# Dropping 16 learned rows behind the token mixers, folding the last token tile, and one ring of 16 slots for all expert weights

## The chip, the cores and the metric

One core of a Trainium2 chip runs the whole program; nothing is computed on the host. The metric is the device time of one execution in microseconds (us). Engines are named as in the profile: PE (TensorE, matmuls), PEld (its weight loads), DVE (VectorE), ACT (ScalarE), POOL (GpSimd), SP (SyncE, which here only issues DMAs, in the order in which they are written).

## What is computed

One layer of a hybrid decoder step, in float32, for one prompt of 256 tokens with 16 learned tokens ahead of it (272 rows), and 8 sample sequences of 8 tokens (64 rows): 336 rows of width 1024.

```
hp = concatenate([meta, x_prompt]);  hs = x_sample
h += W_out( sigmoid(g_A) * P_A(RWKV7(xn)) + sigmoid(g_B) * P_B(FoX(xn)) ),   xn = RMSNorm(h)
hp = hp[:, 16:]                                # the learned rows are dropped here
h += HierMoE(RMSNorm(h))                       # top 1 of 4 groups, then top 2 of its 8 experts
y = RMSNorm(h)
```

Each of the 32 experts is `silu(x @ w1) * (x @ w3) @ w2` with an inner width of 256; its weights are 3 MB (w1 and w3 side by side in two parts, w2 as a third). The learned rows are needed in the mixers (the prompt attends to them, and their keys and states are returned), but nothing behind the mixers returns them.

## The kernel before

The 336 rows are tokens in three tiles, `ROWS = [128, 128, 80]`: tile 0 begins with the 16 learned rows, tile 2 holds the last 16 prompt rows and the 64 sample rows. The program is a row of blocks with a barrier between them: *proj* (projections), *rwkv_pre*, *rwkv* (levels, samples, pairs, chunks), *rwkv_post*, *cache* (attention of the samples over 16 pages each, with 64 MB of page loads), *merge* (from 619 us) and *moe* (from 724 us).

The gates g_A and g_B are 16 blocks of 128 x 336, one for each `gate_mm` (8 float32 matmuls, each two instructions, L222). They are spread over *rwkv_pre* (6), the levels (4), the samples (2), the pairs (2) and *rwkv_post* (2), where they fill gaps on PE; ACT copies each to a stage and SP writes it to `gates_dram`. *cache* reads them back.

*merge*, in PE's order: the merged rows mT (L1910, 8 blocks, `gate` and `obT` against the two projections; DVE multiplies by the sigmoids, POOL adds), then `out_proj(0)`, `out_proj(1)`, `turn_x2(0)`, the first half of `out_proj(2)`, `logits(0)`, `turn_x2(1)`, its second half, `logits(1)`, `turn_x2(2)`, `logits(2)` (L1923, L1939, L1950). On DVE `residual(i)` adds the input (L2042), `norm(i)` makes x2 (L2048 clears the unused rows of tile 2, L2055 multiplies), with the sum of squares and the root on ACT (L1986, L1989). Behind `logits(2)` a chain of some 40 small DVE operations picks the experts, with a mask `tokmask` for the learned rows and the empty ones, and PE counts the tokens of each expert (L1969, L1972).

*moe* takes the experts in 8 quads of 4 (`NQD`, `QE`), with room for 32 tokens each (`CAP`). In PE's order for quad q: `hidden(q, 0)` (L2222, w1 and w3's first half of rows, 4 experts on 32 columns of the array each), `scatter(q-1)` (L2237, the tokens' results into two banks, which DVE adds to h2, L2415), `hidden(q, 1)`, `gather_quad(q+1)` (L2202, x2 by a 0/1 matrix), `outputs(q)` (L2245, L2256, w2). Tokens beyond an expert's 32 are done in passes of one expert each: after `hidden(3, 1)` (`OVQ = 3`) PE, ACT and DVE run `overflow(p)` n_pass times (L2273 to L2299, L2463). n_pass is read from a table that DVE makes at the stage's start (`ovt_ready`).

Loads of the weights. `expert_load(q, part, j)` brings 1 MB into a slot. There are 16 slots; the order is (q, part, j), 12 loads a quad. The first 16 go to slots 0 to 15, 12 of them and (1, 0, j) in *merge*, as its own weights are used up. From the 17th on the slot is `(n - 16) % 12`. Before each load SP waits until the slot's last user is done (`freed`): `w13a_used` or `w13b_used` for parts 0 and 1, the second `y_ps` of the quad for part 2. The pass's loads go to slots 12 to 14 (`ow`), behind (3, 2, 3) in SP's order (L2180).

The end: after the last `outputs` and `scatter(7)` DVE adds, ACT squares, DVE scales (L2503), and SP writes y_p and y_s.

Of the kernel before, what the change touches and what calls it, by code (L numbers as in the profile page):

```python
# [21 lines left out]
NE = NG * EPG  # L22
# [7 lines left out]
ATILES = AP_ // P  # L30
ZC = 1 + LP + DB * (1 + DS)
# [10 lines left out]
MAXOV = 2 * (T - NMETA) // (CAP + 1)  # L42

# [48 lines left out]
def build(nc, A, O):  # L92
# [17 lines left out]
    with ctx:  # L110
# [95 lines left out]
        gates_dram = nc.dram_tensor("gates_dram", (2 * (DM // P), P, T), f32, kind="Internal").ap()  # L206
# [535 lines left out]
        with nc.Block("rwkv_pre") as block:  # L742
# [81 lines left out]
            def _(act):  # L824
                def gate_out(j):
# [3 lines left out]
                    nc.scalar.activation(stage[j % 2], bank[6 + j % 2][:, 0:T], ACT.Copy).then_inc(S("gt_sb"), 1)  # L829
# [158 lines left out]
        with nc.Block("rwkv_pairs") as block:  # L988
# [272 lines left out]
            def _(act):  # L1261
# [19 lines left out]
                def gate_out(j, b):  # L1281
# [4 lines left out]
                    cp(stage[j % 2], bank[b][:, 0:T]).then_inc(S("w_gt_sb"), 1)  # L1286
# [164 lines left out]
        with nc.Block("rwkv_post") as block:  # L1451
# [90 lines left out]
            def _(act):  # L1542
                def gate_out(j):
# [4 lines left out]
                    nc.scalar.activation(stage[j % 2], bank[6 + j % 2][:, 0:T], ACT.Copy).then_inc(S("p_gt_sb"), 1)  # L1548
# [69 lines left out]
        gsb = Space(arena, free_k, mark_k1)(NGT, T)  # L1618
# [213 lines left out]
        mT = sp6(KT, T)  # L1832
        sp6 = Space(arena, free_k, tail - SLOT)
        h2 = sp6(NT, DM)
        mark6 = sp6.at
        sp6.at += NGT * T - NT * DM
        tga, tgb = (sp6(2, T) for _ in range(2))
        mark_t = sp6.at
        xt6 = sp6(NT, DM)
        lnb2 = sp6(DM)  # L1840
        mfills = [f + 16 for f in cache_fills]
# [3 lines left out]
        x2 = sp7(NT, DM)  # L1845
        x2T = xnT
# [5 lines left out]
        tokmask = sp7(NT)  # L1852
# [19 lines left out]
        with nc.Block("merge") as block:  # L1872
            @block.sync
            def _(sp):
                sp.dma_start(xt6[0:NMETA, 0, :], A["meta"]).then_inc(S("xr_in"), 16)
                sp.dma_start(xt6[NMETA:P, 0, :], A["xp"][0:P - NMETA, :]).then_inc(S("xr_in"), 16)
                sp.dma_start(xt6[:, 1, :], A["xp"][P - NMETA:2 * P - NMETA, :]).then_inc(S("xr_in"), 16)
                sp.dma_start(xt6[0:NMETA, 2, :], A["xp"][2 * P - NMETA:SEQ, :]).then_inc(S("xr_in"), 16)
                sp.dma_start(xt6[NMETA:ROWS[2], 2, :], A["xs"]).then_inc(S("xr_in"), 16)
# [11 lines left out]
                for j in range(QE):  # L1891
                    if j < QE - 1:
                        sp.wait_ge(S("out_k"), 2 * j + 2)
                    else:
                        sp.wait_ge(S("ho_ps"), 2 * NT)
# [3 lines left out]
            def _(pe):  # L1899
                for d in range(ND):  # L1900
# [7 lines left out]
                    for a, src in enumerate((gate, obT)):  # L1908
                        for k in range(4):
                            mm = nc.tensor.matmul(bank[b0 + a][:, 0:T], w[:, d % 2, a, k, :], src[:, k, :],  # L1910
                                                  start=(k == 0), stop=(k == 3))
                        mm.then_inc(S("mg_ps"), 1)
                def out_proj(i, ks):
                    r = ROWS[i]
                    for k in ks:
# [6 lines left out]
                        for half in range(2):  # L1922
                            mm = nc.tensor.matmul(bank[2 * i + half][0:r, :], mT[:, k, i * P:i * P + r],  # L1923
                                                  w[:, k % 2, half * 512:(half + 1) * 512],
                                                  start=(k == 0), stop=(k == KT - 1))
                            if k == KT - 1:
                                mm.then_inc(S("ho_ps"), 1)
# [5 lines left out]
                def turn_x2(i):  # L1933
                    n = ROWS[i]
                    pe.wait_ge(S("x2_ready"), i + 1)
                    for half in range(2):
                        for k in range(4):
                            kk = 4 * half + k
                            mm = nc.tensor.transpose(bank[tbank[i] + half][:, k * P:k * P + n],  # L1939
                                                     x2[0:n, i, kk * P:(kk + 1) * P], ident[0:n, 0:n])  # L1940
                        mm.then_inc(S("x2T_ps"), 1)

                def logits(i):
                    n = ROWS[i]
# [15 lines left out]
                out_proj(2, range(KT // 2, KT))  # L1960
                logits(1)
                turn_x2(2)
# [4 lines left out]
                for i in range(NT):  # L1967
                    for k in range(i + 1):
                        nc.tensor.matmul(bank[7][:, i * NE:(i + 1) * NE], tri_tok if k == i else ones, fe(k),  # L1969
                                         start=(k == 0), stop=(k == i))  # L1970
                for k in range(NT):
                    mm = nc.tensor.matmul(bank[7][:, NT * NE:(NT + 1) * NE], ones, fe(k),  # L1972
# [4 lines left out]
            def _(act):  # L1977
# [6 lines left out]
                for i, n in enumerate(ROWS):  # L1984
                    act.wait_ge(S("h2_sb"), 2 * i + 2)
                    nc.scalar.activation(jk[0:n, i, :], h2[0:n, i, :], ACT.Square,  # L1986
                                         accum_out=ss[0:n, i:i + 1]).then_inc(S("ss2"), 1)
# [3 lines left out]
                    nc.scalar.activation(x2T[:, 4:8, i * P:i * P + n],  # L1991
                                         bank[(6, 0, 2)[i] + 1][:, :].rearrange("p (k t) -> p k t", k=4)[:, :, 0:n],
                                         ACT.Copy).then_inc(S("x2T_b"), 1)
# [6 lines left out]
            def _(pool):  # L2000
# [11 lines left out]
                ch(nc.gpsimd.memset(tokmask, 1.0))  # L2012
# [566 lines left out]
```

## Time and profile before

| | |
|---|---|
| three runs | 989.3 us median, 983.65 to 995.3 |
| profiled execution | 986.92 us, of it the span 985.3 |
| PE | busy 819.0 us, 83% of the span |
| DVE, ACT, POOL | 361.7, 188.9, 153.4 us |
| granted PE clock | 0.899 of full |
| DMA | 219.01 MB, mean 222 GB/s |
| expert weights | 99 loads of 1 MB |
| *merge* and *moe* | from 619 us to the end |

Busy shares are means over stages with different limits, so they don't say what bounds the kernel. Readings below are by stretches. A float32 matmul is two instructions in the profile, so a count of x32 is 16 matmuls. Times are from the span's start.

### The profile page before, as it was taken

Reading aid. Unit: us, or ns where it says so; the run is one execution under the profiler, and the core shown is the slowest. Engines: PE = TensorE matmul, PEld = TensorE weight load, DVE = VectorE, ACT = ScalarE, POOL = GpSimd, SP = SyncE. Lnnn points to the kernel's source line nnn. Section 1 sums busy time; section 2 is a strip of 40 time slices with the busy share of each in tenths; the row PEclk is TensorE's granted clock in tenths of the full one; section 3 lists DMA queues with packets and bytes.
Section 4 is the critical chain, followed back from the end, with each engine's and each line's share of the span. In section 5 each row is a group of like instructions: output and inputs, shape, how many; then the busy total and the mean of one; then the engine's idle time right before and its main releaser. Section 6 shows DMA issues by size and latency. Waiting matters only on the chain. (4 is left out here: it accounts for less than half of the span.)

```text
span 985.3 us, 20675 instructions
## 1 busy us (share of the span) xinstructions
PE 819.0 (83%) x8683; PEld 489.6 (50%) x8683; DVE 361.7 (37%) x666; ACT 188.9 (19%) x430; POOL 153.4 (16%) x299
## 2 busy tenths in 40 slices
PE   4999899989689898666586886899769997899885
PEld 2445566655566577433364554564454444444321
DVE  2002433379422443548675640112352221422223
ACT  3003121143312110221131121301111110111012
POOL 8200110060400200500344443120000000000000
PEclk9999899979789699787878897899869998999998
DMA  8422232213203032166999999962409999399993
GB/s 332 180 85 89 86 102 80 86 39 114 78 21 103 10 92 69 60 197 210 376 415 413 396 380 388 365 252 89 171 1 407 421 422 424 160 391 420 422 422 124
DMA packets 48694, 219.01 MB, mean 222 GB/s; under 512 B 17567, under 2 KB 21962, under 8 KB 24026
## 3 DMA queue, kind: packets, MB, share of 16 engines
q1 hardware_dynamic: 41440, 186.03, 49.0%
q0 software_dynamic: 6512, 31.48, 8.2%
q8 instruction: 68, 1.11, 0.4%
q10 hardware_dynamic: 650, 0.18, 0.1%
q14 instruction: 24, 0.20, 0.1%
HBM read 210.96 MB, written 6.70 MB: 221 GB/s over the span
## 5 line engine op out<-in xcount | busy, mean ns | idle before, releaser
L222 PE MATMUL bank<-arena 128*128 128x336 f32 x256 | 85.7, 477 | 4.0 <-PEq L108 4.0
L2415 DVE TENSOR_TENSOR arena<-arena,bank 128x512 f32<-128x512 f32 (+1 forms) x48 | 32.9, 686 | 122.4 <-PE bank L2237 121.7
L1448 DVE STREAM_TRANSPOSE arena<-arena 128x2048 f32<-128x2048 f32 x32 | 72.3, 2289 | 10.0 <-DMA arena<-in_ck 8.9
L197 POOL DMA_DIRECT2D arena<-in_cv x112 | 58.0, 518 | 105.1 <-PE bank L1711 76.4
L495 PE MATMUL bank<-arena 128*128 128x336 f32 x224 | 70.4, 470 | 4.4 <-DVE arena L641 4.4
L2222 PE MATMUL bank<-arena 128*32 128x512 f32 x512 | 66.7, 608 | 7.2 <-DMA arena<-in_w_exp 6.5
L1711 PE MATMUL bank<-arena 128*16 128x128 f32 x1024 | 41.4, 329 | 33.9 <-issue 16.5
L2202 PE MATMUL bank<-arena 128*128 128x128 f32 x432 | 56.1, 294 | 9.7 <-DVEq L2452 5.6
L2202 PEld LDWEIGHTS bank<-arena 128*128 128x128 f32 x432 | 54.4, 209 | 16.6 <-issue 7.2
L222 PEld LDWEIGHTS bank<-arena 128*128 128x128 f32 x256 | 48.3, 199 | 27.7 <-issue 8.9
L474 PE MATMUL bank<-arena 128*128 128x512 f32 (+1 forms) x144 | 62.1, 593 | 0.0
L1670 PE MATMUL bank<-arena 32*32 32x512 f32 x1024 | 46.8, 737 | 17.0 <-DVE arena L1448 8.6
L495 PEld LDWEIGHTS bank<-arena 128*128 128x128 f32 x224 | 43.6, 199 | 27.2 <-issue 9.5
L1711 PEld LDWEIGHTS bank<-arena 128*16 128x16 f32 x1024 | 33.9, 115 | 39.9 <-DMA arena<-in_cv 18.3
L1262 ACT ACTIVATE arena<-bank 128x384 f32<-128x384 f32 (+6 forms) x63 | 26.1, 445 | 126.7 <-PE bank L222 47.4
L2237 PE MATMUL bank<-arena 128*128 128x512 f32 x96 | 46.9, 618 | 0.6 <-ACT arena L2375 0.6
L1910 PE MATMUL bank<-arena 128*128 128x336 f32 x128 | 39.5, 473 | 4.7 <-PEq L108 4.7
L474 PEld LDWEIGHTS bank<-arena 128*128 128x128 f32 (+1 forms) x144 | 25.4, 177 | 35.9 <-issue 35.8
L2222 PEld LDWEIGHTS bank<-arena 128*32 128x32 f32 x512 | 18.0, 111 | 49.0 <-issue 34.2
L1923 PE MATMUL bank<-arena 128*128 128x512 f32 (+1 forms) x96 | 41.7, 592 | 0.0
L2329 ACT ACTIVATE arena<-bank 128x512 f32<-128x512 f32 x36 | 21.5, 598 | 102.6 <-PE bank L2202 68.5
L1670 PEld LDWEIGHTS bank<-arena 32*32 32x32 f32 x1024 | 21.7, 116 | 35.6 <-issue 14.4
(458 smaller groups left out, 1072.4 us busy)
## 6 DMA issues: line engine op xcount, KB each, us to landing
arena<-in_w_exp SPq DMA_DIRECT2D x99, 1024.0 KB, 16.7
arena<-in_ck SPq DMA_DIRECT2D x128, 256.0 KB, 6.4
arena<-in_cv POOLq DMA_DIRECT2D x112, 256.0 KB, 8.0
arena<-in_w_gate SPq DMA_DIRECT2D x8, 1024.0 KB, 4.9
arena<-in_w_za SPq DMA_DIRECT2D x7, 1024.0 KB, 6.8
arena<-in_w_zb SPq DMA_DIRECT2D x6, 1024.0 KB, 13.1
arena<-in_cv SPq DMA_DIRECT2D x16, 256.0 KB, 3.3
arena<-in_w_proj SPq DMA_DIRECT2D x4, 1024.0 KB, 20.7
```

The source lines that it names most:

```text
L197: eng.dma_start(tile[n:P:4, :], src[bass.ds(page, 1)].rearrange("a (p j) n -> (a p) (j n)", j=4))\
L222: mm = nc.tensor.matmul(bank[b][:, 0:T], w[:, k, a, :], xnT[:, k, :], start=(k == 0), stop=(k == KT - 1))
L474: mm = nc.tensor.matmul(bank[q % 6][0:n, :], xnT[:, k, i * P:i * P + n], w[:, k % 4, :], start=(k == 0), stop=(k == KT - 1))
L495: mm = nc.tensor.matmul(bank[j % 2][:, 0:T], w[:, k, (j % 2) * P:(j % 2 + 1) * P], xnT[:, k, :], start=(k == 0), stop=(k == KT - 1))
L1448: return nc.vector.transpose(kT[b % 2][:, :, 128 * m:128 * m + 128].rearrange("p j (n k) -> p n j k", n=4), slot[m].rearrange("p (n j k) - ...
L1670: nc.tensor.matmul(bank[i][32 * g:32 * g + 32, :], qs[r, b, j, :], kT[b % 2][r, j, :], start=(t == 0), stop=False)
L1711: mm = nc.tensor.matmul(bank[7][32 * g:32 * g + 2 * DS, 0:P], pT[:, n, 2 * DS * g:2 * DS * (g + 1)], page_part(slot[4 + m], n % 4)[:, g * ...
L1910: mm = nc.tensor.matmul(bank[b0 + a][:, 0:T], w[:, d % 2, a, k, :], src[:, k, :], start=(k == 0), stop=(k == 3))
L1923: mm = nc.tensor.matmul(bank[2 * i + half][0:r, :], mT[:, k, i * P:i * P + r], w[:, k % 2, half * 512:(half + 1) * 512], start=(k == 0), s ...
L2202: mm = nc.tensor.matmul(bank[half][:, k * P:(k + 1) * P], x2[:, i, kk * P:(kk + 1) * P], lhs_sel[:, i, :], start=(i == 0), stop=(i == NT - 1))
L2222: mm = nc.tensor.matmul(bank[2][j * CAP:(j + 1) * CAP, :], xg[:, q % 2, k, j * CAP:(j + 1) * CAP], wslot[s][:, (k % 4) * 512:(k % 4 + 1) * ...
L2237: nc.tensor.matmul(bank[6 + half][:, :], gT[:, i, :], yg[:, half * 512:(half + 1) * 512], start=True, stop=True).then_inc(S("ys_ps"), 1)
```

## The change

1. Behind the mixers only the 320 rows that are returned are kept: `TM = T - 16`, `TROWS = [128, 128, 64]`. Gates, merged rows, output projection, x2 and all of *moe* have 320 columns; tile 0 is the first 128 prompt rows, tile 2 the 64 sample rows. `tokmask` goes.
2. The last tile is folded: its 64 rows of 1024 stand as 128 partitions of 512, the left half of each row on partitions 0 to 63 (`UP`), the right half on 64 to 127 (`DN`). h2, x2 and the input have 5 pieces of 512 instead of 6. `out_proj(2)` writes both halves into one bank, on 64 columns of the array each; `gather` takes the folded tile first, by halves of the rows; `scatter` writes it as one piece; additions are 5 instead of 6. The row's sum of squares is added over the two halves by a matmul with `pair`.
3. One ring for the loads. All 16 slots are used again in turn, and the overflow pass's three loads have a place in the order, ahead of (3, 2, 0).

```diff
-        stage = [arena[:, NF - (2 - i) * T:NF - (1 - i) * T] for i in range(2)]
+        stage = [arena[:, NF - (2 - i) * T:NF - (2 - i) * T + TM] for i in range(2)]
...
-                mm = nc.tensor.matmul(bank[b][:, 0:T], w[:, k, a, :], xnT[:, k, :], start=(k == 0), stop=(k == KT - 1))
+                mm = nc.tensor.matmul(bank[b][:, 0:TM], w[:, k, a, :], xnT[:, k, NMETA:T], start=(k == 0), stop=(k == KT - 1))
...
-        QUAD, FIRST = 3 * QE, len(wslot)
+        FIRST = len(wslot)
+
+        OVQ = 3
+        ring = [(q, part, j) for q in range(NQD) for part in range(3) for j in range(QE)]
+        at = ring.index((OVQ, 2, 0))
+        ring[at:at] = [(NQD, part, 0) for part in range(3)]
 
         def load_slot(q, part, j):
 
-            n = QUAD * q + QE * part + j
-            return n if n < FIRST else (n - FIRST) % QUAD
+            return ring.index((q, part, j)) % FIRST
...
-                            mm = nc.tensor.matmul(bank[2 * i + half][0:r, :], mT[:, k, i * P:i * P + r],
-                                                  w[:, k % 2, half * 512:(half + 1) * 512],
+                            out = bank[2 * i + half][:, :] if i < NT - 1 else bank[4][(UP, DN)[half], :]
+                            mm = nc.tensor.matmul(out, mT[:, k, i * P:i * P + r],
+                                                  w[:, k % 2, half * HALF:(half + 1) * HALF],
                                                   start=(k == 0), stop=(k == KT - 1))
...
+                def pair_sums(name, b, col):
+                    pe.wait_ge(S(name), NT)
+                    nc.tensor.matmul(bank[b][:, col:col + 1], pair, ss[:, NT - 1:NT], start=True, stop=True)\
+                        .then_inc(S("pair_ps"), 1)
...
                     for k in range(KT):
-                        mm = nc.tensor.matmul(bank[lbank[i]][0:n, 0:E_], x2T[:, k, i * P:i * P + n], wr[:, k, :],
-                                              start=(k == 0), stop=(k == KT - 1))
+                        for r in (slice(0, P),) if i < NT - 1 else (UP, DN):
+                            mm = nc.tensor.matmul(bank[lbank[i]][r, 0:E_], x2T[:, k, i * P:i * P + n], wr[:, k, :],
+                                                  start=(k == 0), stop=(k == KT - 1))
...
+                pe.wait_ge(S("rconst"), 1)
                 logits(1)
+                pair_sums("ss2", 5, 0)
                 turn_x2(2)
                 logits(2)
...
-                    if i == NT - 1:
-                        ch(nc.vector.memset(x2[:, i, :], 0.0))
...
-            pq, pp_, _ = [order[m] for m in range(n) if load_slot(*order[m]) == load_slot(q, part, j)][-1]
+            pq, pp_, _ = ring[ring.index((q, part, j)) - FIRST]
+            if pq == NQD:
+                return S("o_over"), 1
             return (S(used[pp_]), pq + 1) if pp_ < 2 else (S("y_ps"), 2 * pq + 2)
...
-                for q, part, j in order[FIRST:]:
+                for q, part, j in ring[FIRST:]:
                     sp.wait_ge(*freed(q, part, j))
-                    expert_load(sp, q, part, j)
-                    if (q, part, j) == (OVQ, 2, QE - 1):
-                        sp.wait_ge(S(used[0]), 2)
+                    if q < NQD:
+                        expert_load(sp, q, part, j)
+                    elif part == 2:
                         sp.wait_ge(S("ovt_ready"), 1)
                         n_pass = sp.value_load(np_i[0:1, 0:1], min_val=1, max_val=MAXOV)
...
+                    for k in range(4):
+                        for half, r in enumerate((UP, DN)):
+                            nc.tensor.matmul(bank[half][:, k * P:(k + 1) * P], x2[r, NHT - 1, k * P:(k + 1) * P],
+                                             lhs_sel[r, NT - 1, :], start=(k == 0), stop=False)
...
+                def spread(n, dst):
+
+                    i, half = divmod(n, 2)
+                    if i < NT - 1:
+                        return nc.tensor.matmul(dst[:, :], gT[:, i, :], yg[:, half * HALF:(half + 1) * HALF],
+                                                start=True, stop=True)
+                    for half, r in enumerate((UP, DN)):
+                        mm = nc.tensor.matmul(dst[r, :], gT[:, i, r], yg[:, half * HALF:(half + 1) * HALF],
+                                              start=True, stop=True)
+                    return mm
...
                         with pe.Fori(0, n_pass) as p:
                             overflow(p)
+                        pe.sem_inc(S("o_over"), 1)
```

## Rows read from the trace of the kernel before

**Rows 1.** The page's slices of 24.6 us: GB/s moved.
```profile
GB/s 332 180 85 89 86 102 80 86 39 114 78 21 103 10 92 69 60 197 210 376 415 413 396 380 388 365 252 89 171 1 407 421 422 424 160 391 420 422 422 124
```

**Rows 2.** Windows of 5 us: each engine's busy time, granted clock, DMA share, GB/s.
```profile
710.00:715.00 5.00, 2.32 (x16) 2.21 (x16) 1.78 (x10) 1.79 (x3) 0.00 (x0) 0.50 0.00 0
...
735.00:740.00 5.00, 5.00 (x52) 1.56 (x48) 0.00 (x0) 0.81 (x1) 0.00 (x0) 1.00 0.09 16
...
800.00:805.00 5.00, 3.92 (x30) 0.92 (x27) 0.00 (x0) 0.00 (x0) 0.00 (x0) 1.00 1.02 424
...
845.00:850.00 5.00, 4.49 (x11) 2.12 (x12) 2.75 (x4) 0.36 (x1) 0.00 (x0) 1.00 0.35 146
...
860.00:865.00 5.00, 5.00 (x47) 1.50 (x43) 0.00 (x0) 1.58 (x3) 0.00 (x0) 1.00 0.30 79
...
915.00:920.00 5.00, 4.18 (x25) 1.11 (x26) 0.00 (x0) 0.00 (x0) 0.00 (x0) 0.66 1.02 424
...
960.00:965.00 5.00, 2.54 (x8) 0.48 (x8) 0.42 (x1) 0.39 (x1) 0.00 (x0) 1.00 0.94 386
```

**Rows 3.** Expert loads: the page's DMA issues; SP's line of the overflow pass.
```profile
arena<-in_w_exp SPq DMA_DIRECT2D x99, 1024.0 KB, 16.7
...
L2180 SPq DMA_DIRECT2D arena<-in_w_exp x3: 333/357/1026, 802.4 to 804.1; - x3
```

**Rows 4.** Chain that ended last, in order of time: start, us, what.
```profile
845.51 5.41 PE bank L2299 x12
...
850.94 0.69 DVE arena L2463
...
852.24 5.61 PE bank L2202 x48
...
858.79 3.64 PE bank L2256 x32
...
872.29 3.57 PE bank L2222 x32
```

**Rows 5.** Timeline of PE in merge: start, us, line, shapes, count, wait.
```profile
619.17 39.49 PE L1910 MATMUL bank<-arena 128*128 128x336 f32 x128 [4.70 <-PEq L108]
658.50 27.63 PE L1923 MATMUL bank<-arena 128*128 128x512 f32 x64
...
686.84 7.03 PE L1923 MATMUL bank<-arena 128*80 128x512 f32 x16
...
708.49 1.33 PE L1939 MATMUL bank<-arena 80*128 80x80 f32 x8 [3.44 <-DVE arena L2055]
710.44 2.32 PE L1950 MATMUL bank<-arena 128*80 128x36 f32 x16 [0.62 <-ACT arena L1991]
...
725.66 8.22 PE L2202 MATMUL bank<-arena 128*128 128x128 f32 x48 [2.77 <-DVEq L2396]
```

**Rows 6.** Timeline of DVE in merge and at the start of moe.
```profile
689.38 1.28 DVE L2055 SCALAR_TENSOR_TENSOR arena<-arena 128x1024 f32<-128x1024 f32 x1
...
705.53 0.91 DVE L2048 MEMSET arena<- 128x1024 f32 x1 [1.46 <-ACT arena L1986]
...
707.16 1.28 DVE L2055 SCALAR_TENSOR_TENSOR arena<-arena 80x1024 f32<-80x1024 f32 x1
...
732.64 0.17 DVE L2441 TENSOR_SCALAR arena<-arena 128x6 f32<-128x6 f32 x1
```

**Rows 7.** Timeline of PE in the levels, one of 16 filler pieces.
```profile
282.41 1.40 PE L222 MATMUL bank<-arena 128*128 128x336 f32 x4
283.74 0.87 PE L1084 MATMUL bank<-arena 32*32 32x64 f32 x48
```

**Rows 8.** Timeline of PE in rwkv_pre: matmuls on two halves of the rows.
```profile
211.19 1.68 PE L786 MATMUL bank<-arena 64*128 64x336 f32 x5
...
213.38 1.57 PE L791 MATMUL bank<-arena 64*128 64x336 f32 x5
```

**Rows 9.** Timeline of DVE at the end.
```profile
980.33 1.28 DVE L2503 SCALAR_TENSOR_TENSOR arena<-arena 80x1024 f32<-80x1024 f32 x1
```

More of the change, by code:

```diff
@@ L1831, in build @@
         sp6 = Space(arena, free_o - NPAIR * T, free_k)
-        mT = sp6(KT, T)
+        mT = sp6(KT, TM)
         sp6 = Space(arena, free_k, tail - SLOT)
-        h2 = sp6(NT, DM)
+        NHT = 2 * NT - 1
+        h2 = sp6(NHT, HALF)
         mark6 = sp6.at
-        sp6.at += NGT * T - NT * DM
-        tga, tgb = (sp6(2, T) for _ in range(2))
+        sp6.at += NGT * TM - NHT * HALF
+        tga, tgb = (sp6(2, TM) for _ in range(2))
         mark_t = sp6.at
-        xt6 = sp6(NT, DM)
+        xt6 = sp6(NHT, HALF)
         lnb2 = sp6(DM)
+        lnb3 = sp6(HALF)
+        pair, tri2 = sp6(P), sp6(P)
+        UP, DN = slice(0, P // 2), slice(P // 2, P)
         mfills = [f + 16 for f in cache_fills]
@@ L2011, in _ @@
                 ch(nc.gpsimd.memset(one32, 1.0))
-                ch(nc.gpsimd.memset(tokmask, 1.0))
-                for pat, b, m in (([[P, NT]], -NMETA, 1), ([[-P, NT]], T - 1, -1)):
-                    ch(nc.gpsimd.affine_select(out=tokmask, in_=tokmask, compare_op=ALU.is_ge, fill=0.0, base=b,
-                                               pattern=pat, channel_multiplier=m))
+                for n in range(2):
+                    h = slice(n * P // 2, (n + 1) * P // 2)
+                    ch(nc.gpsimd.tensor_tensor(pair[:, h], ident[:, UP], ident[:, DN], add))
+                    ch(nc.gpsimd.tensor_copy(tri2[:, h], tri_tok[:, UP]))
                 pool.sem_inc(S("rconst"), 1)
@@ L2231, in scatter @@
                     pe.wait_ge(S("yg_sb"), 2 * q + 2)
-                    for i in range(NT):
-                        for half in range(2):
-                            m = 6 * q + 2 * i + half
-                            if i:
-                                pe.wait_ge(S("hacc"), m - 1)
-                            nc.tensor.matmul(bank[6 + half][:, :], gT[:, i, :], yg[:, half * 512:(half + 1) * 512],
-                                             start=True, stop=True).then_inc(S("ys_ps"), 1)
+                    for n in range(NHT):
+                        if n >= 2:
+                            pe.wait_ge(S("hacc"), NHT * q + n - 1)
+                        spread(n, bank[6 + n % 2]).then_inc(S("ys_ps"), 1)
                 def outputs(q):
@@ L2296, in overflow @@
                     pe.wait_ge(S("o_yg_sb"), p * 2 + 2)
-                    for i in range(NT):
-                        for half in range(2):
-                            nc.tensor.matmul(bank[ybank[2 * i + half]][:, :], gT[:, i, :],
-                                             yg[:, half * 512:(half + 1) * 512],
-                                             start=True, stop=True).then_inc(S("o_ys_ps"), 1)
+                    for n in range(NHT):
+                        spread(n, bank[ybank[n]]).then_inc(S("o_ys_ps"), 1)
                     pe.wait_ge(S("o_done"), p + 1)
@@ L2321, in _ @@
                 scatter(NQD - 1)
+                pe.wait_ge(S("ss3"), NT)
+                nc.tensor.matmul(bank[5][:, 0:1], pair, ss[:, NT - 1:NT], start=True, stop=True)\
+                    .then_inc(S("pair_f"), 1)
             @block.scalar
@@ L2458, in overflow @@
                     nc.vector.tensor_tensor(ohid, ohid, bank[2][:, FF:2 * FF], mult).then_inc(S("o_hid"), 1)
[L2459 to L2464 removed]
+                    for n in range(NHT):
+                        dve.wait_ge(S("o_ys_ps"), p * NHT + n + 1)
+                        ch(nc.vector.tensor_tensor(h2[:, n, :], h2[:, n, :], bank[ybank[n]][:, :], add))
                     dve.sem_inc(S("o_done"), 1)
```

207 lines of the change are left out of this document (104 added, 103 removed).

## The prediction

> **What bounds the kernel now.** I began with the page's slices and looked for the stretch in which one resource is full. From about 740 us on the transfers run at some 420 GB/s in nearly every slice [rows 1]; before that TensorE or a chain through several engines sets the pace, with transfers at a tenth to a half of that rate (the cache stage, at 390 to 415 GB/s, excepted). So the kernel has two regimes, and I read each by another view.
>
> From 740 us I used the table by 5 us windows. A share of the full rate in a window tells when the stream began or stopped in it: 16 GB/s in 735:740 means 0.2 us of transfer, so the stream starts at 739.8. By the same step it stops at 846.7, starts again at 864.1 and ends at 964.6 [rows 2]. The page counts 99 loads of the expert weights, three of them for one overflow pass [rows 3]. 16 loads fit before the stage, so 83 remain: 43 (40 and the three of the pass) in 106.9 us, which is 2.49 us each, and 40 in 100.5 us, 2.51 us each. The stage from 740 to 965 is therefore 83 loads in a row with one hole of 17.4 us. TensorE is not the bound there: from one gather, 852.24, to the next, which follows L2222's end at 872.29 + 3.57 = 875.86, it needs 23.6 us, and the twelve loads of a quad need 30 us [rows 4].
>
> The hole has its cause in the ring. The first 16 loads fill 16 slots, but after them only 12 are used again. Load (4,2,0) needs the slot of (3,2,0), which is free only when outputs(3) is done, and that stands behind the overflow pass and gather(4): 862.4, when L2256 ends [rows 4]. The stream starts 1.7 us after it.
>
> Before 740 us the stream waits for hidden(0,0), thus for the whole chain ahead: PE L1910 and L1923 back to back from 619 to 686, the third tile's 7.03 us (two such pieces, of which one row stands), then norm(2), the router, and a gather of 8.22 us [rows 5]. All 16 slots are full by 710 (710:715 moves nothing [rows 2]), so every microsecond gained in this chain starts the stream a microsecond earlier.
>
> **The change, part by part.** Times before are of the profiled execution (986.9 us, span 985.3).
>
> Gates. 16 of 336 columns go. In L1910, 128 instructions take 39.49 us, 0.3085 us each; L1923 with 512 columns takes 27.63/64 = 0.4317 [rows 5]. Between the two that is 0.70 ns a column, 0.84 if all of the 0.4317 goes by columns. 16 columns are 11 to 13.5 ns. Of the 256 gate instructions 128 sit as filler in the chains of the levels, samples and pairs, where PE runs without a gap (four of them, then small matmuls at once [rows 7]); the others lie beside a busy VectorE. 128 x 13.5 ns = 1.7 us at most, 3.5 us if all 256 counted, 0 if the chains behind the filler are the limit. I take 1.2.
>
> Merge. 128 x 13.5 ns = 1.7 us; 1.4 by the lower slope, 39.49 x 16/336 = 1.9 by the share. It is on the path.
>
> Output projection of the third tile. 32 instructions of 80 columns and 512 moving elements take 2 x 7.03 = 14.06 us one after another [rows 5]. Now each half of the output goes to its own 64 columns of the array. Do two such halves run side by side? With four groups of 32 columns they do: 32 instructions of L2222 in 3.57 us, 0.11 us each, though one alone would take 0.43 [rows 4, 5]. With two halves of the rows too: L786 and L791, 8 instructions each with 336 columns, run from 211.19 to 214.95, 3.8 us, where 16 x 0.3085 would be 4.9 [rows 8]; the overlap is only where both are queued. So I take 7.0 us saved (0 if they don't overlap). It moves the end: turn_x2(1) between the two parts needs x2 of tile 1 from VectorE, ready at 690.7 [rows 6], and PE would come to it at 692, still after that.
>
> norm(2). Before, one cleared x2 (0.91 us on the path) and multiplied 1024 wide, 1.28 us [rows 6]. Now there is one residual addition on the path, a square and a multiply half as wide (about 0.5 and 0.6 less) and no clearing, but the row's halves must be added on TensorE: pair_sums stands behind logits(1), 1.9 us after the projection's end, and costs some 0.4. From the projection's end to x2 I work out 3.7 us against 5.1 before: 1.4 saved. Bounds: 0.9, the clearing alone, and 1.6.
>
> turn_x2(2) and logits(2). Transposes and their copies: 1.33 us before for eight [rows 5], four now, 0.5 less. The logits take 16 instructions of 80 columns in 2.32 us [rows 5], at half clock (0.50 in 710:715 [rows 2]); now 32 of 64 columns. If their time goes by loaded columns that is 2.32 x 128/80 = 3.7, so 1.4 more; at full clock half of it, 1.9, 0.4 less. Between 0.9 lost and 0.9 saved I take 0. The router loses one operation: 0.2.
>
> gather. 48 instructions become 32 of full height and 16 of half height. If the latter run in pairs, as the row halves of [rows 8], a sixth goes: 5.61/6 = 0.9 us [rows 4] at full clock, 1.4 at half clock, 0 if not. I take 0.9 for gather(0), 0.9 for the overflow's and 0.9 for gather(4). Six other gathers save the same and it costs and brings nothing, as PE waits for loads there.
>
> Switches of the array's form. Four L222 need 4 x 0.3085 = 1.23 us, and start to start they take 1.33 before the 32x32 ones follow [rows 7]: 0.1 us a switch. Some seven are new on the path before 740, three behind: 0.7 and 0.3 lost. The Trainium skill, TensorEngine Tiling (Array Packing), section Key Properties, says that changing the tiling mode drains the engine, which speaks against this change; it gives no price, and the row's 0.1 us is small, so by rule and row alike it trims the gain and does not turn it.
>
> POOL makes pair and tri2 right after the merge, which ends near 658.5 [rows 5]; logits(1) waits for them some 38 us later, so they cost nothing (if they were late, logits(1) and all behind would be). SP issues eight loads at the stage's start instead of seven, 0.4 us, beside a running merge. Nothing.
>
> So hidden(0,0), and with it the stream, comes 1.2 + 1.7 + 7.0 + 1.4 + 0 + 0.2 + 0.9 - 0.7 = 11.7 us earlier.
>
> The ring. Its order is now 44 expert loads, the pass's three, then (3,2,*) and on, each in the slot of the load 16 earlier. By that rule (4,2,0) takes the slot of (3,1,3), free before the pass; (4,2,1) to (4,2,3) take the slots of (3,1,3)'s followers, the pass's three, free at o_over; (5,0,0) takes that of (3,2,0), free at outputs(3). In the frame of before: 44 loads instead of 43 bring the stream to 849.2. The pass ended at 851.6; with the overflow's gather 0.9 shorter and its scatter a sixth of L2299's 5.41, 0.9 [rows 4], it ends at 849.8, less 0.2 for switches, and 2 us later three loads follow (7.5 us, to about 859). outputs(3) ends at 862.4 - 2.7 + 0.3 = 860.0, and the stream restarts at 861.7 with 36 loads left instead of 40: 861.7 + 36 x 2.51 = 952.1 against 964.6. Gain 12.5: four loads, 10.1, and 2.4 from the earlier restart. PE needs about 21.7 us a quad then, so it stays behind no load: four quads from 860 end near 942. SP issues the pass's loads ahead of (3,2,*); queued behind its wait for ovt_ready are those four loads and all later ones, but that semaphore comes at 732.8 [rows 6], some 50 us before. hidden(3,1) sets the pass's start and not the pass's own weights.
>
> Tail. The third tile has one addition instead of two (0.7, L2463 in [rows 4] shows the size) and a multiply half as wide (1.28 to 0.65 [rows 9]). The new matmul for the sum lies under result(1). 1.3 saved, 0.6 to 2.0. y_s leaves in two transfers where there were one of y_p and one of y_s: even.
>
> Sum: 11.7 + 12.5 + 1.3 = 25.5, so 961.4 for an execution like the profiled one. That one lies 2.4 us under the median of three (983.65 to 995.3), so I place the forecast halfway, at **963 us**.
>
> **Rivals.** (a) *Halves of the array don't overlap.* 7.0 in the projection, three gathers and one scatter (3.6) are lost: 963 + 10.6 = 974. For it: no row shows 64-column halves with 128 rows. Against it: rows show four column groups and two row groups side by side. 0.08.
>
> (b) *The hole stays.* The last SP wait before the next full run of loads is still outputs(3), and if o_over doesn't let three loads through (SP late, or the stream not yet dry) only the 2.4 remains: 973. For it: SP issues strictly in order. Against: o_over comes 10 us ahead of outputs(3). 0.12.
>
> (c) *More than worked out:* all gate columns count (2.3 more), logits at full clock (0.9), tail 2.0, projection's neighbours too: 957. 0.12.
>
> (d) *Slower: the clock.* The loads already outlast PE's work in a quad by 6 us; with 21.7 us of work, waits grow to 8. After one of them the granted clock was 0.66 in 915:920 [rows 2], between its levels of 1.2 and 2.4 GHz. If it stayed at the lower level, a quad's work would be 43.4 us, above the 30 of its loads: 13.4 x 7 quads = 94 lost, 963 + 94 = 1057. It decides from 33.6 us a quad on (25/7 beyond 30), so when 12 of the 21.7 us run at half clock. Against it: 800:805 holds a wait for a load too (3.92 us busy of 5) and stayed at 1.00 [rows 2]. The Trainium skill, TensorE: Matmul & The Clock Gate, section HAM oscillation, describes a kernel that waits for a DMA in every tile and is cold after each; in this trace one window of a wait agrees (0.66) and the other does not (1.00). 0.03.
>
> The forecast itself: 0.65, with its own range of 957 to 969.
>
> **Numbers.** The range 954 to 975 takes in (a), (b), (c) and the spread of the runs and leaves (d) and the rest. About 1% (10 us) is what a measurement of this kernel can tell. Only (d) and mishaps of size end above 979: faster 0.94, same 0.03, slower 0.03.
>
> **What the changed profile would show.** L1910 near 37.8 us; L1923's third tile about 7 us in all instead of 14.06; a first expert load behind the gather at about 726.6 instead of 738.3; transfers without a hole to about 837.5, then two holes of 2 to 3 us around three loads, and the last load landing near 940; TensorE waiting for loads in every later quad. I would be wrong if the third tile's projection still took 14 us, if one hole of 15 us stood there, or if the granted clock were under 1 for whole quads.

## The result and the profile after

| | before | after |
|---|---|---|
| median | 991.5 us (4 runs) | 960.9 us (4 runs) |
| spread | 983.65 to 995.3 | 955.93 to 964.77 |
| profiled span | 985.3 | 954.3 |

The ratio is 0.9694, 95% interval 0.9656 to 0.9732: 3% faster, 30.6 us by the medians, 31.0 us between the two profiled spans.

The stream of expert loads first, as in [rows 2]. Windows of the changed kernel: span, busy time of PE, PEld, DVE, ACT, POOL with counts, granted clock, DMA share, GB/s.

```profile
720.00:725.00 5.00, 5.00 (x52) 1.44 (x44) 0.00 (x0) 0.00 (x0) 0.00 (x0) 1.00 0.35 92
...
830.00:835.00 5.00, 3.50 (x29) 2.01 (x28) 4.11 (x10) 0.00 (x0) 0.00 (x0) 1.00 0.79 292
835.00:840.00 5.00, 4.26 (x42) 3.42 (x44) 2.97 (x6) 1.47 (x3) 0.00 (x0) 1.00 1.02 428
840.00:845.00 5.00, 5.00 (x51) 1.51 (x44) 0.00 (x0) 1.58 (x3) 0.00 (x0) 1.00 0.64 215
...
935.00:940.00 5.00, 4.07 (x29) 1.21 (x29) 0.00 (x0) 1.01 (x2) 0.00 (x0) 1.00 0.19 54
```

By the same step as before, the stream starts at 723.7 (739.8), has two holes of about 1.5 and 2.4 us where one of 17.4 was, and ends at 935.6 (964.6). 83 loads in 211.9 - 3.9 us are 2.51 us each, as before. The windows read a few tenths short at the end. The chain that ended last has the last load's landing itself, at 941.85 + 23.54 = 965.39 before and at 907.79 + 28.11 = 935.90 now:

```profile
941.85 23.54 DMA arena<-in_w_exp
```

```profile
907.79 28.11 DMA arena<-in_w_exp
```

The chain ahead of it, on PE, beside [rows 5]: start, us, line, shapes, count, and the wait before it.

```profile
616.43 36.11 PE L1930 MATMUL bank<-arena 128*128 128x320 f32 x128 [3.32 <-PEq L112]
652.38 27.63 PE L1944 MATMUL bank<-arena 128*128 128x512 f32 x64
...
680.82 3.65 PE L1944 MATMUL bank<-arena 128*64 128x512 f32 x16
...
692.60 0.36 PE L1965 MATMUL bank<-arena 128*128 128x1 f32 x2
694.49 1.11 PE L1959 MATMUL bank<-arena 128*128 128x128 f32 x4 [1.53 <-DVE arena L2084]
696.17 1.93 PE L1976 MATMUL bank<-arena 128*64 128x36 f32 x32 [0.57 <-ACT arena L2022]
...
711.24 2.08 PE L2222 MATMUL bank<-arena 64*128 64x128 f32 x16 [2.80 <-DVEq L2431]
713.25 4.61 PE L2227 MATMUL bank<-arena 128*128 128x128 f32 x32
```

The third tile's projection takes 3.65 us a part instead of 7.03 (the second of two such parts, at 687.21, takes 3.65 too). L1965 is the new matmul that adds the two halves of a row's sum.

And the end of the program, beside [rows 9], the folded tile's multiply on DVE:

```profile
949.58 0.15 DVE L2529 TENSOR_SCALAR arena<-bank 128x1 f32<-128x1 f32 x1
950.06 0.16 DVE L2534 RECIPROCAL arena<-arena 128x1 f32<-128x1 f32 x1 [0.33 <-ACT arena L2418]
950.26 0.75 DVE L2537 SCALAR_TENSOR_TENSOR arena<-arena 128x512 f32<-128x512 f32 x1
```

0.75 us instead of 1.28. From the last load's landing to the span's end it is 18.4 us, 19.9 before.

PE behind the holes waits for no load for two quads. The second halves of quads 4, 5 and 6 (`hidden(q, 1)`, 32 instructions each), then the first half of quad 7:

```profile
851.52 3.65 PE L2259 MATMUL bank<-arena 128*32 128x512 f32 x32
...
873.52 3.64 PE L2259 MATMUL bank<-arena 128*32 128x512 f32 x32
...
895.51 4.13 PE L2259 MATMUL bank<-arena 128*32 128x512 f32 x32
...
913.41 1.05 PE L2259 MATMUL bank<-arena 128*32 128x512 f32 x2 [1.44 <-DMA arena<-in_w_exp]
```

That is 22.0 us a quad against 30 for its twelve loads. The stream stood still until 844 because every slot that was free had been filled, so PE comes to quad 4 with its loads far ahead of it and catches up with them only in quad 7, near 910.

### The profile page after: what moved, and what is told of

Read it like the earlier page. It is cut to its first block and busy times, and to the rows that moved or that the text cites. A ratio compares the mean times of both kernels' runs of the same rounds, so it can differ in the third digit from the quotient of the medians.

```text
span 954.3 us, 20697 instructions
## 1 busy us (share of the span) xinstructions
PE 790.9 (83%) x8699; PEld 473.0 (50%) x8699; DVE 352.6 (37%) x653; ACT 186.6 (20%) x430; POOL 153.7 (16%) x300
## 5 line engine op out<-in xcount | busy, mean ns | idle before, releaser
L226 PE MATMUL bank<-arena 128*128 128x320 f32 x256 | 82.8, 467 | 4.2 <-PEq L112 4.2
L503 PE MATMUL bank<-arena 128*128 128x336 f32 x224 | 70.9, 472 | 4.2 <-DVE arena L649 4.2
L2259 PE MATMUL bank<-arena 128*32 128x512 f32 x512 | 67.3, 610 | 6.8 <-DMA arena<-in_w_exp 6.1
L2448 DVE TENSOR_TENSOR arena<-arena,bank 128x512 f32<-128x512 f32 x40 | 27.5, 688 | 116.3 <-PE bank L2236 113.3
L482 PE MATMUL bank<-arena 128*128 128x512 f32 (+1 forms) x144 | 62.1, 593 | 0.0
L226 PEld LDWEIGHTS bank<-arena 128*128 128x128 f32 x256 | 48.6, 201 | 25.6 <-issue 9.5
L503 PEld LDWEIGHTS bank<-arena 128*128 128x128 f32 x224 | 43.8, 200 | 27.2 <-issue 9.7
L1719 PEld LDWEIGHTS bank<-arena 128*16 128x16 f32 x1024 | 33.4, 114 | 39.5 <-DMA arena<-in_cv 20.4
L2259 PEld LDWEIGHTS bank<-arena 128*32 128x32 f32 x512 | 16.7, 111 | 50.8 <-issue 37.3
L1930 PE MATMUL bank<-arena 128*128 128x320 f32 x128 | 36.1, 445 | 3.3 <-PEq L112 3.3
L2290 PE MATMUL bank<-arena 128*32 128x512 f32 x256 | 31.8, 595 | 7.6 <-ACT arena L2404 5.7
L2227 PE MATMUL bank<-arena 128*128 128x128 f32 x288 | 37.2, 291 | 0.0
L2236 PE MATMUL bank<-arena 128*128 128x512 f32 x72 | 35.3, 617 | 1.4 <-ACT arena L2364 0.8
L2227 PEld LDWEIGHTS bank<-arena 128*128 128x128 f32 x288 | 35.5, 204 | 1.3 <-issue 0.4
```

What stands on the lines that cost most here:

```text
L226: mm = nc.tensor.matmul(bank[b][:, 0:TM], w[:, k, a, :], xnT[:, k, NMETA:T], start=(k == 0), stop=(k == KT - 1))
L482: mm = nc.tensor.matmul(bank[q % 6][0:n, :], xnT[:, k, i * P:i * P + n], w[:, k % 4, :], start=(k == 0), stop=(k == KT - 1))
L503: mm = nc.tensor.matmul(bank[j % 2][:, 0:T], w[:, k, (j % 2) * P:(j % 2 + 1) * P], xnT[:, k, :], start=(k == 0), stop=(k == KT - 1))
L1719: mm = nc.tensor.matmul(bank[7][32 * g:32 * g + 2 * DS, 0:P], pT[:, n, 2 * DS * g:2 * DS * (g + 1)], page_part(slot[4 + m], n % 4)[:, g * ...
L1930: mm = nc.tensor.matmul(bank[b0 + a][:, 0:TM], w[:, d % 2, a, k, :], src[:, k, NMETA:T], start=(k == 0), stop=(k == 3))
L2227: mm = nc.tensor.matmul(bank[half][:, k * P:(k + 1) * P], x2[:, 2 * i + half, k * P:(k + 1) * P], lhs_sel[:, i, :], start=False, stop=(k = ...
```

## The experiments

Each was timed beside runs of the kernel before. The changed kernel is 0.9694 of it. The stream's start and end come from windows of 2 us, read in the same way, and by the landings in the chain the ends come 0.3 to 1.3 us later (e3 942.8, e5 936.0, e9 930.8), so a length is good to about 1 us. The length leaves out what differs ahead of it, and I rely on it where a run's median is blurred by the spread of some 9 us between runs.

| run | median, ratio | stream: start, end, length | idle in it |
|---|---|---|---|
| before | 991.5 | 739.8, 964.9, 225.1 | 17.4 |
| changed | 960.9, 0.9694 | 723.7, 935.2, 211.5 | 3.9 |
| e1 fold only | 972.4, 0.9794 | 729.5, 951.2, 221.7 | 13.5 |
| e2 ring only | 980.9, 0.9894 | 739.2, 953.6, 214.4 | 7.4 |
| e3 pass's loads behind | 967.1, 0.9777 | 723.2, 941.8, 218.6 | 11.6 |
| e5 17 slots | 955.9, 0.9661 | 729.1, 935.7, 206.6 | 1.8 |
| e6 scatter twice | 960.6, 0.9680 | 727.3, 939.6, 212.3 | 5.0 |
| e9 18 slots | 951.0, 0.9589 | 725.9, 929.5, 203.6 | 1.2 |

**The two halves apart (e1, e2).** e1 goes back to the loads of before in the changed kernel, e2 puts the new ring into the kernel before. The core of e1:

```diff
-            return ring.index((q, part, j)) % FIRST
+            n = QUAD * q + QE * part + j
+            return n if n < FIRST else (n - FIRST) % QUAD
...
-                    if q < NQD:
-                        expert_load(sp, q, part, j)
-                    elif part == 2:
+                    expert_load(sp, q, part, j)
+                    if (q, part, j) == (OVQ, 2, QE - 1):
+                        sp.wait_ge(S(used[0]), 2)
```

> The changed kernel with the loads of before: 12 slots used again, the pass's loads behind (3,2,3). Theory (the ring is worth the four loads that the hole kept back, 4 x 2.51 = 10.1 us, and the fold the rest): 10 us slower than the changed kernel, 971; one hole of about 17.4 - 2.4 = 15 us in the stream of loads in front of the last 40; the stream starts as early as in the changed kernel (723.7 us). Rival (the ring brings nothing of its own): 961. Rival (the gain is nearly all the ring's): 985 or more.

> The kernel before with the one ring alone; all 336 rows and three tiles as they were. Theory: 10 us faster than the kernel before, ratio 0.990; the stream starts at about 739.8 as before, two holes of about 2.5 and 3 us around three loads. Rival (the hole stays, since outputs(3) lets the stream go on): ratio 0.998 to 1.000 with one hole of 15 us.

e1: 972.4 us, ratio 0.9794 (0.9744 to 0.9844). e2: 980.9, ratio 0.9894 (0.9856 to 0.9932). The ring alone brings 1.1% (10.5 us), the fold and the dropped rows alone 2.1% (20.4 us), and 3.1% together: the parts add up within their intervals of about 0.4%. The hole in e1 and the two in e2, windows cut to them:

```profile
836.00:850.00 14.00, 11.76 (x102) 6.68 (x105) 6.84 (x16) 3.06 (x6) 0.00 (x0) 1.00 0.09 22
```

```profile
848.00:853.00 5.00, 3.52 (x18) 2.03 (x17) 4.11 (x11) 0.00 (x0) 0.00 (x0) 1.00 0.25 70
861.00:864.00 3.00, 3.00 (x31) 0.94 (x27) 0.00 (x0) 0.98 (x2) 0.00 (x0) 1.00 0.29 101
```

In e1 (first) the transfers run at 22 GB/s for 14 us while PE is 84% busy with the rest of the pass, gather(4) and outputs(3). In e2 they stop for 4.7 and 2.8 us, longer than in the changed kernel, since the pass of the unfolded tiles takes longer: 31.5 us from its gather to gather(4), 28.6 in the changed kernel.

**The place in the ring (e3).** 16 slots in one ring, but the pass's loads behind (3,2,3):

```diff
-        at = ring.index((OVQ, 2, 0))
+        at = ring.index((OVQ + 1, 0, 0))
```

> The changed kernel with 16 slots in one ring, but the pass's three loads behind (3,2,3) instead of ahead of (3,2,0). Theory (the place decides who frees the slots of (4,2,1) to (4,2,3): the pass, or outputs(3) ten us later): only one load more than with the old ring goes ahead of outputs(3), 39 loads are left instead of 36, so 7.5 us slower than the changed kernel, 968.5, with one hole of some 12 us. Rival (16 slots instead of 12 are what counts, the place is even): 961.

967.1 us, ratio 0.9777 (0.9717 to 0.9837), one hole of 11.6 us, stream 7.1 us longer than in the changed kernel (7.4 by the landings). Only the order of seven loads differs. So of the ring's gain the place is worth some 7 us and the four more slots the other 3: (4,2,1) to (4,2,3) get slots that the pass frees, and not slots that outputs(3) frees ten us later. Its hole:

```profile
832.00:844.00 12.00, 10.53 (x100) 6.50 (x104) 5.25 (x13) 3.05 (x6) 0.00 (x0) 1.00 0.12 32
```

**Two halves of the array side by side (e4, e10).**

```diff
-                            out = bank[2 * i + half][:, :] if i < NT - 1 else bank[4][(UP, DN)[half], :]
+                            out = bank[2 * i + half][:, :] if i < NT - 1 else bank[4 + half][UP, :]
```

> The changed kernel, but both halves of the third tile's output projection on the same 64 columns of the array (the second goes to another bank, and the right halves of the sample rows get what lay in the bank, so y_sample is not the reference's). Same count of instructions. Theory (7 us of the gain are the two halves side by side): the 32 instructions take 14 us instead of 7.3, all behind starts 7 us later, 968. Rival (the chain behind is set by VectorE and ScalarE): under 2 us slower.

1001.3 us, ratio 1.0112 (1.0067 to 1.0157): 40 us slower, and neither theory had that. The projection itself did as expected, in both of its parts:

```profile
681.30 7.08 PE L1944 MATMUL bank<-arena 128*64 128x512 f32 x16
...
691.12 7.08 PE L1944 MATMUL bank<-arena 128*64 128x512 f32 x16
```

and from merge's start to the stream's start e4 takes 114.3 us against 107.3. The other 33 us came behind: a hole from 808 to 841, and this row of its DMA issues:

```profile
arena<-in_w_exp SPq DMA_DIRECT2D x102, 1024.0 KB, 20.4
```

102 loads instead of 99: the right halves of the sample rows held other data, the router chose by them, and there were two passes of three loads. e10 repeats it with the number of passes held to one.

> Run e4 with the number of overflow passes held to one, so that its changed router inputs don't bring a second (one pass's tokens are left out, y_sample is not the reference's). Theory: the 7.4 us by which e4's stream of loads started later are all that the two halves side by side are worth, 968. Rival (e4's 40 us are the projection's): 985 or more.

966.5 us, ratio 0.9747 (0.9710 to 0.9784), 99 loads, stream as long as the changed kernel's (211.5), start 114.4 us behind merge's. So 7 us is what the two column halves side by side give, and e4's total says nothing on them. The medians differ by 5.6 us.

**What a second pass costs (e7, e8).** That accident is a case of its own: the pass's loads stand ahead of (3,2,*) in SP's queue, and the second pass's loads wait for the first pass.

```diff
-                    ch(TS(novt, pbi, 1.0, None, vmax))
+                    ch(TS(novt, pbi, 2.0, None, vmax))
```

> The changed kernel with at least two overflow passes; the second selects no row and adds zeros, so the results are the same. Run e4 had a second pass by its changed router inputs: 1001 us and a hole of 32 us. Theory (SP waits for the first pass's end before it issues the second's loads, and (3,2,*) and all loads behind stand in that queue, so the stream stops while both passes run): some 34 us slower than the changed kernel, 994, with one hole of about 32 us from 802 to 834. Rival (e4's extra time had another cause): within 12 us of the changed kernel.

> The same two passes, with the loads of before (12 slots used again, the pass's loads behind (3,2,3)), beside e1 as its one-pass case. Theory: the stream has four more loads ahead of SP's wait, so it stops 10 us later than in e7, but (4,0,*) and (4,1,*) now stand behind the wait too: about 30 us above e1, 1001, so with two passes the old ring is 5 to 10 us behind the new one, no more ahead of it. Rival (with two passes the place ahead of (3,2,0) costs more than the ring brings): e8 at or under e7.

e7: 995.8 us, ratio 1.0043 (1.0018 to 1.0067), 34.9 us over the changed kernel. e8: 1005.1, 32.7 over e1. SP in e7: the six loads of the two passes, and only then (3,2,0):

```profile
774.49 60.58 SPq L2201 DMA_DIRECT2D arena<-in_w_exp  x6
835.29 15.94 SPq L243 DMA_DIRECT2D arena<-in_w_exp  x13
```

```profile
804.00:834.00 30.00, 23.99 (x89) 13.80 (x89) 6.28 (x13) 3.54 (x7) 0.00 (x0) 0.89 0.00 1
```

30 us at 1 GB/s. In sum e7's stream has a hole of 33.5 us there where the changed kernel's holes are 3.9: 29.6 us more of idle time, and three more loads are 7.5. With the old ring (e8) there are two holes, 23.5 and 16 us, where e1 had one of 13.5. Both pay some 33 us for a pass, and the new ring keeps its 9 us. The rival of e8 fell: the place ahead of (3,2,0) is not the worse one with two passes. With this loop of loads in SP's queue, which is served in order, a second pass costs about its whole length either way.

**Is PE's work behind the hole worth anything (e6)?**

```diff
+                        if q in (4, 5, 6):
+                            spread(n, bank[6 + n % 2])
                         spread(n, bank[6 + n % 2]).then_inc(S("ys_ps"), 1)
```

> The changed kernel with the scatter's matmuls of quads 4, 5 and 6 done twice (same results into the same banks): 4.9 us more of PE work in each of three quads. Theory (behind the hole the stream of loads sets the pace and PE has 8 us to spare a quad): no change, 961, the last load lands at the same time; so the shorter gathers and scatters of these quads brought nothing either. Rival (PE's work counts): 14 us slower, 975.

960.6 us, ratio 0.9680 (0.9635 to 0.9725). The lines of PE from 735 us on, e6 and then the changed kernel, x counts are instructions:

```profile
L2236 PE MATMUL bank<-arena 128*128 128x512 f32 x96 | 44.9, 607 | 1.4 <-ACT arena L2366 0.8 <-ACT arena L2412 0.6
```

```profile
L2236 PE MATMUL bank<-arena 128*128 128x512 f32 x72 | 35.3, 617 | 1.4 <-ACT arena L2364 0.8 <-ACT arena L2410 0.6
```

9.6 us more here, some 2.6 in L2239, and the stream 0.8 us longer, with 1.1 us more idle: nothing lost that can be measured. The 8 us that a quad of loads takes longer than PE's 22.0 hold these 4 us a quad. So the shorter gathers and scatters of quads 4 to 6 brought nothing either. Those of the pass and gather(4) stand in the chain ahead of outputs(3); no run took them apart.

**More slots (e5, e9).** e5 keeps the 0/1 matrices of three quads instead of eight and gets room for a 17th slot, filled in merge behind residual(2). e9 adds an 18th over the norm weights' room, filled behind norm(2); the last norm's weights then go into the slot of (7,0,0).

```diff
-        gsel = Space(arena, mark7, mark_t + NHT * HALF)(NQD, NT, P)
+        gsel = Space(arena, mark7, mark_t + NHT * HALF)(3, NT, P)
...
+                sp.wait_ge(S("h2_sb"), NHT)
+                expert_load(sp, 1, 1, 0)
+                sp.wait_ge(S("x2_ready"), NT)
+                expert_load(sp, 1, 1, 1)
...
+        last0 = wslot[load_slot(NQD - 1, 0, 0)]
+        lnb2, lnb3 = last0[:, 0:DM], last0[:, DM:DM + HALF]
```

> The changed kernel with a 17th slot, in room won by keeping the 0/1 matrices of three quads instead of eight; load (1,1,0) goes there in merge, behind residual(2). Theory (from 724 us on the time is the count of loads left, 2.51 us each, and the holes): the stream starts at the same time with 82 loads left instead of 83, 2.5 us faster than the changed kernel, 958.4; the first hole is gone, the second is as before or shorter. Rival (the chain of PE or the tail sets the end): no change, 961.

> The 17-slot kernel with an 18th, in the room of the norm weights, which at the end are read into the slot of (7,0,0) instead; load (1,1,1) goes there in merge behind norm(2). Theory (each load brought ahead of 724 us is worth its 2.51 us): 81 loads left, one more load's time off, 2.5 us faster than 17 slots and 5 faster than the changed kernel, 953.5 to 956. Rival (the holes' end, outputs(3), now sets the rest, or the tail waits for the norm weights): no faster than 17 slots.

e5: 955.9 us, ratio 0.9661 (0.9624 to 0.9698). e9: 951.0, ratio 0.9589 (0.9556 to 0.9623), 4.1% faster than the kernel before and 1% faster than the changed one. By the stream's length they win 4.9 and 7.9 us over the changed kernel: 2.51 a slot, as expected, and most of the rest is idle time within the stream that went, 2.1 and 2.7 (3.9 to 1.8 and to 1.2). The landings give 5.3 and 7.3. Each further slot also covers a part of the holes. I had left that out. e9's stream, and the one dip in it (0.6 us of idle time within it):

```profile
728.00:842.00 114.00, 100.27 (x660) 48.45 (x657) 30.36 (x60) 16.37 (x34) 0.00 (x0) 0.96 1.01 423
842.00:844.00 2.00, 2.00 (x19) 0.65 (x21) 0.00 (x0) 0.92 (x2) 0.00 (x0) 1.00 0.85 291
844.00:929.00 85.00, 79.20 (x555) 32.03 (x547) 19.09 (x32) 11.07 (x23) 0.00 (x0) 0.99 1.01 423
```

81 loads at 423 GB/s are nearly all there is from 726 to 930; to win more there, loads have to move ahead of 726 or go.

**The gates (e11).** The changed kernel with `xnT[:, k, :]` and 336 columns in `gate_mm` again.

> The changed kernel with the gates' matmuls over all 336 columns again; what is copied and stored stays 320. The blocks ahead of merge took 1.4 us (rwkv_pre) and about 2.4 us (the next three) less in four kernels with the narrow gates than in two with the wide. Theory (all 256 instructions count, at 13.5 ns each): rwkv_pre takes 47.2 us again instead of 46.0 and the stretch from its end to merge 367.7 instead of 365.3. Rival (the narrower copies and transfers did it): as with the narrow gates.

One run, 964.6 us in all. From the first matmul of rwkv_pre to the first of the next block: 47.3 us, against 46.0 in the changed kernel and 45.8 to 46.1 in nine other kernels with narrow gates, and 47.2 and 47.5 in the two with the gates of before. A piece of 16 gate instructions in e11, then in the changed kernel:

```profile
215.97 4.80 PE L226 MATMUL bank<-arena 128*128 128x336 f32 x16
```

```profile
215.35 4.57 PE L226 MATMUL bank<-arena 128*128 128x320 f32 x16
```

0.23/16 = 14 ns an instruction. The rest of the way to merge took 369.5 us against 367.7 expected and 365.8 in the changed kernel. The theory holds in sign and for rwkv_pre in size; the later stretch varies by itself (364.4 to 368.6 with narrow gates), so its size isn't settled by one run.

## Why the prediction was right, step by step

963 us was forecast and 960.9 measured, and 25.5 us of gain between executions like the profiled ones, where 31.0 came. The mechanism held in each part but one picture, PE's waits for loads, on which the sum did not rest. Gates and merge were too small, and about half of what was missing there is a difference between executions, which no term had. So 963 lies nearer to the median of 960.9 than the working deserves: between the profiled executions the sum is 5.5 us short.

| term | forecast | measured |
|---|---|---|
| blocks ahead of merge (gates) | 1.2 | 2.7 (619.17 to 616.43) |
| merge, L1910 | 1.7 | 3.4 (39.49 to 36.11) |
| third tile's projection | 7.0 | 6.8 (14.06 to 7.30) |
| norm(2) | 1.4 | 1.5 (5.1 to 3.6) |
| turn_x2(2), logits(2) | 0 | 0.7 (4.3 to 3.6) |
| router up to the gather | 0.2 | -0.2 |
| gather(0) | 0.9 | 1.6 (8.22 to 6.6) |
| switches of the array's form | -0.7 | -0.4 beside the third tile's parts, the others within the above |
| *start of the stream* | *11.7* | *16.1* |
| four loads and earlier outputs(3) | 12.5 | 13.4 (by the last load's landing; 12.9 by windows of 5 us) |
| tail, from that landing on | 1.3 | 1.5 |

The last three, start, loads and tail, make 25.5 and 31.0.

**Gates: mis-sized.** The step that failed is "the others lie beside a busy VectorE", worth nothing. rwkv_pre's 96 gate instructions gave 1.4 us, 14 ns each, all of it: PE ran without a gap there, and a busy VectorE beside it did not mean that VectorE was waited for. I had looked at VectorE's share (9.5 of 10 us) and not at who waited. Over all kernels the stretch from rwkv_pre to merge took 415.0, 415.1 and 416.9 us with wide gates (before, e2, e11) and 411.8 in the mean of ten with narrow ones, 410.2 to 414.5. That fits the 3.5 us of all 256 instructions, but only rwkv_pre's share is clear of the scatter.

**Merge: the width was right, the clock came on top.** From one of DVE's multiplies to the next but one, which is 16 matmul instructions, PE takes 4.31 us where it took 4.53, 13.8 ns an instruction, 1.7 us in all as forecast. The other 1.7 is the start: PE comes out of a barrier at half clock, and in the profile of before it stayed there until about 625.3, 6.1 us, in that of after until about 619.3, 3 us; the 3.2 us less at half clock are 1.6 us of work. The windows from both, before and then after:

```profile
618.00:620.00 2.00, 0.83 (x2) 0.64 (x3) 0.00 (x0) 0.86 (x1) 0.00 (x0) 0.62 0.97 410
620.00:622.00 2.00, 2.00 (x5) 1.22 (x4) 0.00 (x0) 1.99 (x4) 0.00 (x0) 0.50 1.05 440
622.00:624.00 2.00, 2.00 (x5) 1.22 (x4) 0.00 (x0) 2.00 (x4) 0.00 (x0) 0.50 0.99 264
```

```profile
616.00:618.00 2.00, 1.56 (x3) 1.17 (x4) 0.00 (x0) 1.59 (x2) 0.00 (x0) 0.50 1.00 422
618.00:620.00 2.00, 2.00 (x6) 1.28 (x5) 0.00 (x0) 2.00 (x4) 0.00 (x0) 0.67 1.03 434
620.00:622.00 2.00, 2.00 (x9) 1.36 (x9) 0.49 (x1) 2.00 (x4) 0.00 (x0) 1.00 0.97 399
```

No edit of the change reaches into that; from merge's start to the stream it took 107.3 to 109.3 us in nine kernels with the folded tile's halves side by side. The merge of before took 120.6 us in its own profile and 118.3 in e2, where PE left the half clock after 3.2 us. Against e2 the other eight folded ones gain 10.2 us in their mean (108.1), where 10.5 was forecast for this stretch, and the two profiles 13.3. So up to 3 us of the profiled gain are luck.

**Projection.** Right, and by e10 for the reason given. Rival (a) is out. **logits(2):** the bounds held; 32 instructions of 64 columns took 1.93 us at half clock where 16 of 80 took 2.32, so these too run in pairs, and their time does not go by loaded columns. **gather:** the half-height instructions take 1.09/16 = 0.07 us each at full clock against 0.12 for full height, so they overlap partly: 4.87 us a gather instead of 5.57, 0.7 saved and not 0.9. gather(0), which begins at half clock, gained more. The Trainium skill, TensorEngine Tiling (Array Packing), says in Key Properties that a change of mode drains the engine; the trace agrees, and the price is small. Beside the third tile's projection, which now is on 64 columns, the turn ahead takes 0.97 and 1.00 us start to start where it took 0.87 and 0.91, and the logits behind it 1.81 where they took 1.70: 0.1 us a switch, as the row said. At L2222 to L2227 no gap can be told.

**Ring.** The four loads, the two holes' places and their sizes came as worked out (2 to 3 us each forecast, 1.5 and 2.4 found), and e3 shows that the place and not only the number of slots does it. Rival (b) is out. **The clock, rival (d):** it did not come, but its premise was wrong too. The prediction had waits for loads in every later quad, growing to 8 us. PE waited for none in quads 4 and 5; its waits for expert loads at L2259 were five from 735 us on, 6.1 us in sum, the longest 1.4 (6.5 in five before, at L2222 there), and one of 1.9 at L2290. So (d) was not put to the test that it describes. The window 915:920, behind two of these waits, again shows 0.66, all others from 830 to 950 show 1.00. One wait did cost something, and neither the prediction nor its rows name it: ahead of the overflow pass PE stands for 5.63 us, in both kernels, while DVE makes the pass's 0/1 matrices (L2479 to L2485), and then runs at half clock:

```profile
804.54 2.08 PE L2222 MATMUL bank<-arena 64*128 64x128 f32 x16 [5.63 <-DVEq L2485]
806.55 5.69 PE L2227 MATMUL bank<-arena 128*128 128x128 f32 x32
```

```profile
805.00:810.00 5.00, 5.00 (x32) 4.78 (x31) 0.00 (x0) 0.00 (x0) 0.00 (x0) 0.50 1.01 426
```

The same gather takes 1.16 and 3.84 us in quad 4, so the half clock costs 2.8 us here. The Trainium skill, TensorE: Matmul & The Clock Gate, section HAM oscillation, tells of a kernel that waits for a DMA in every tile and is cold after each. The 5.63 us and the 0.50 agree with it; on waits for loads in every quad this trace can't speak, since there are none. **Tail:** 1.5 us instead of 1.3. The multiply (0.53) and the dropped addition (0.6) came as worked out, and the other 0.4 lies behind DVE's last multiply, in the last transfers (3.7 to 3.3 us to the span's end).

## What to carry to other kernels

Where a stream of loads sets the pace, count the loads that are left when it starts and ask of each hole who frees the slot it waits for: here the order of seven loads was worth 7 us, each further slot 2.5 us and a part of the holes, and PE's work in the quads behind the hole nothing. Look also at what stands ahead of the work that frees a slot: DVE's matrices for the pass (4.2 us) need only a table that is ready some 80 us earlier, and DVE is idle for 4.67 us just ahead of the wait behind which they are placed. Made there, they would start the pass and end both holes earlier, by at most the 3.9 us that the holes last (an estimate; no run tried it). Two halves of one tile on separate columns of the array took nearly the time of one here (3.65 us against 7.08 in e4). An experiment that changes data can change the control flow behind it, so look at a count (here 102 loads) before its time is explained.

## What the runs showed of the hardware

- SP's own issue of a load takes 0.43 us in the median of both kernels, but it can be slow: up to 2.5 us before, and about 2.1 us one after the other at the end of the changed kernel's stream, with more loads under way. In its chain, right before the issue of the last load:

```profile
903.42 2.13 SPq L243
905.55 0.04 issue
905.60 2.14 SPq L243
```

  The last load needs 28.1 us, the time of 11 loads, from issue to landing. It looks as if some 11 or 12 loads of 1 MB can be under way and the next issue waits for one to end; no run tested that apart. It cost nothing, since the stream was full.
- The first block (proj) ended 5.9 us later in three profiles (e1, e5, e8: rwkv_pre began at 210.6) than in the others (204.2 to 205.9), with the same instructions. In e5 PE's clock from 75 to 95 us was 0.85 against 0.91. That may be a part of the spread between runs (956 and 957 or 964 and 965 in the changed kernel), but not all: e6's profiled run of 962.7 us had its rwkv_pre begin at 205.6. It is a reason to compare stretches and not spans.
- Behind an idle stretch of PE its granted clock was half: 0.50 in 805:810 behind 5.63 us of idle time, and at merge's start, for 3 to 6 us.
